# Two transformer blocks on one core: new order of VectorE's and ScalarE's work between stages and at the entry of the HGRN stage

## What is computed

```python
h = norm(x) * (1.0 + scale) + shift        # layer_norm behind stages 0 and 1, rms_norm behind 2 to 6
# stage 0: token_mixer (sparse attention and convolution), then layer_norm(ALPHA * x + gate * y)
# stage 1: swiglu, then layer_norm(ALPHA * x + gate * y)
# stages 2, 4, 5, 7: x + 0.5 * gate * ((silu(h @ w_a) * (h @ w_b)) @ w_down)
# stage 3: x + gate * diff_attention(h);  stage 6: x + gate * hgrn2(h)
```

## Time and profile before

| | us |
|---|---|
| median of 3 runs | 1468.14 (1464.91 to 1470.73) |
| profiled execution | 1470.92 |
| its span, first to last instruction | 1469.2 |
| mean granted TensorE clock | 0.979 of full |

### The profile page before, as it was taken

The page is one execution under the profiler, slowest core; times in us unless marked ns, Lnnn a source line. Parts: engine busy times, 40 slices in busy tenths (PEclk is TensorE's granted clock), DMA queues, the critical chain, the costliest instruction groups (busy, mean ns, idle before and its releaser), DMA issues.

```text
span 1469.2 us, 19939 instructions
## 1 busy us (share of the span) xinstructions
PE 1425.0 (97%) x7214; PEld 1194.3 (81%) x7214; DVE 1061.4 (72%) x1133; ACT 693.4 (47%) x897; POOL 183.4 (12%) x273
## 2 busy tenths in 40 slices
PE   8998899999899999999999999999999999899998
PEld 8897788888788888767788887888888988788887
DVE  5888867775678877776667775688866888755555
ACT  2452354343444435666644345534347856544342
POOL 3103211110301210221101101111101001100000
PEclk7996999999999999999999999999999999999999
DMA  9836478986389995532589983899955342366761
GB/s 354 316 138 201 145 257 308 314 308 213 100 294 341 374 379 170 174 138 91 176 274 313 313 281 111 285 335 341 342 177 171 116 141 87 129 201 211 231 225 62
DMA packets 187528, 335.64 MB, mean 228 GB/s; under 512 B 9170, under 2 KB 123454, under 8 KB 187217
## 3 DMA queue, kind: packets, MB, share of 16 engines
q1 hardware_dynamic: 160528, 237.95, 48.1%
q0 software_dynamic: 26736, 96.71, 18.3%
q10 hardware_dynamic: 208, 0.23, 0.0%
HBM read 332.23 MB, written 2.63 MB: 228 GB/s over the span
## 4 chain that ended last, share of the span: by engine, by line
PE 79%; DVE 10%; issue 4%; ACT 3%; POOL 1%; DMA 1%; SPq 1%; DVEq 0%; ACTq 0%; POOLq 0%
PE ps L2087 70%; DVE wlo L1259 2%; PE ps L2279 1%; PE ps L2095 1%; PE ps L2540 1%; POOL st L492 1%; DVE ada_acc L1560 1%; PE ps L2210 1%; DVE xn L1321 1%; DMA big<-in_w_ada 1%; DVE xs L1327 1%; ACT whi L672 1%; PE ps L2638 0%; PE ps L2755 0%; ACT xn L712 0%
## 5 line engine op out<-in xcount | busy, mean ns | idle before, releaser
L1259 DVE TENSOR_TENSOR wlo<-raw,whi 128x2048 fp32r<-128x2048 f32 x206 | 470.2, 2285 | 153.5 <-ACT whi L672 152.3
L672 ACT ACTIVATE whi<-raw 128x2048 fp32r<-128x2048 f32 x215 | 409.7, 1909 | 213.9 <-PE ps L2087 158.2
L2087 PE MATMUL ps<-whi,hhi 128*128 128x512 f32 (+1 forms) x1208 | 491.2, 407 | 15.7 <-DVE hlo L1307 5.5
L2087 PE MATMUL ps<-whi,hlo 128*128 128x512 f32 (+1 forms) x1208 | 476.4, 394 | 0.0
L2087 PE MATMUL ps<-wlo,hhi 128*128 128x512 f32 (+1 forms) x1208 | 475.9, 394 | 0.0
L2087 PEld LDWEIGHTS ps<-whi,hhi 128*128 128x128 f32 x1208 | 230.2, 191 | 67.8 <-issue 10.2
L2087 PEld LDWEIGHTS ps<-whi,hlo 128*128 128x128 f32 x1208 | 230.0, 190 | 49.6
L2087 PEld LDWEIGHTS ps<-wlo,hhi 128*128 128x128 f32 x1208 | 230.4, 191 | 45.1 <-issue 1.7
L2087 PE MATMUL ps<-whi,ahi 128*128 128x512 f32 x400 | 156.1, 390 | 0.0
L2087 PE MATMUL ps<-whi,alo 128*128 128x512 f32 x400 | 155.7, 389 | 0.0
L2087 PE MATMUL ps<-wlo,ahi 128*128 128x512 f32 x400 | 155.7, 389 | 0.0
(11 more groups left out here) (287 smaller groups left out, 1494.9 us busy)
## 6 DMA issues: line engine op xcount, KB each, us to landing
raw<-in_ffn_w_in SPq DMA_DIRECT2D x176, 512.0 KB
ada_raw<-in_ada_w POOLq DMA_DIRECT2D x96, 512.0 KB, 5.1
raw<-in_ffn_w_down SPq DMA_DIRECT2D x44, 1024.0 KB
big<-in_ada_w POOLq DMA_DIRECT2D x48, 512.0 KB, 6.3
raw<-in_hgrn_w_in SPq DMA_DIRECT2D x16, 1024.0 KB
raw<-in_attn_w_qkv SPq DMA_DIRECT2D x12, 1024.0 KB
ada_raw<-in_w_ada POOLq DMA_DIRECT2D x23, 512.0 KB, 5.0
raw<-in_w_gate SPq DMA_DIRECT2D x22, 512.0 KB
```

Of the source, the lines that this page charges most:

```text
L672: sc.activation(whi[:, slot, 0:n], raw[:, slot, 0:n], ACT.Copy).then_inc(w_hi, 1)
L1259: ve.tensor_tensor(wlo[:, slot, 0:n], raw[:, slot, 0:n], whi[:, slot, 0:n].bitcast(F32), ALU.subtract)\
L2087: done = pe.matmul(dst, lhsT, rhs, start=first and n == 0, stop=final and n == 2, skip_group_check=True)
```

## The change

- Border of stages 1 and 2: the column sums of stage 2 leave the last gate-up product of stage 1 and take the place of 16 filler products behind `close`; `leave_second` is a new order for VectorE, with the layer norm's first passes ahead of the wait for the root; the mean for the root is added on VectorE for both halves (`whole_mean`); ScalarE makes the high part of the second unit ahead of the squares and modulates all eight tiles in both halves.
- All borders: ScalarE alone modulates the second half, all eight tiles. `SHARED` lists the halves that stay divided.
- Borders from 2 on: the high parts of border units come in halves (`hi_half`) at other places in ScalarE's order, TensorE waits for low parts in halves (`lo_first`, then `w_lo`).
- Stages 3 and 6: the first transposes of the next stage go ahead of the last down product of half 1 instead of into its middle.
- Entry of stage 6: ScalarE makes two high parts first, then copies the gate row, then the exponential. VectorE makes two low parts ahead of `bounds`.
- Filler products in `enter`: 16 at stage 2 before the second transposes (9 and 8 around them before), 5 or 1 instead of 7 at the others.

The lines of the diff, with most of the context left out:

```diff
+SHARED = tuple((s, 0) for s in (1, 3, 4, 5, 6, 7))
+HALVED = [FIRST[s] + g for s in range(3, NSUB) for g in range(2) if g or s in (4, 7)]
...
     def inverse_rms(s, t):
         mean = st[:, 1 + 2 * t:2 + 2 * t]
-        if t:
-            pool.wait_ge(mean_eps, s)
+        if t or s == 1:
+            pool.wait_ge(mean_eps, s + t)
             inverse_root(mean, 1, rms_root)
             return
         pool.wait_ge(sums_s, 4 * (s - 1) + 2)
...
             sc.wait_ge(w_used, used(unit - RING, lap))
         sc.activation(whi[:, slot, 0:n], raw[:, slot, 0:n], ACT.Copy).then_inc(w_hi, 1)
+    h_mod_s_count = [NT]
+    def hi_half(unit, h):
+        slot, cols = unit % RING, slice(h * D, (h + 1) * D)
+        if h == 0:
+            sc.wait_ge(w_land[slot], 32 * (unit // RING + 1))
+            sc.wait_ge(w_used, used(unit - RING))
+        sc.activation(whi[:, slot, cols], raw[:, slot, cols], ACT.Copy).then_inc(w_hi if h else hi_first, 1)
     def modulate(s, t):
-        sc.wait_ge(h_tr, 4 * s + 2 * t + 2)
         toks = slice(t * P, (t + 1) * P)
+        shared = (s, t) in SHARED
         for g in range(2):
-            for kt in (4 + 2 * g, 5 + 2 * g):
-                done = sc.activation(hf[:, kt, toks], ps[:, 2 * t + 1, (kt - 4) * P:(kt - 3) * P], ACT.Identity,
+            if shared:
+                kts = (4 + 2 * g, 5 + 2 * g)
+                if g == 0:
+                    sc.wait_ge(h_tr, 4 * s + 2 * t + 2)
+            else:
+                kts = range(4 * g, 4 * g + 4)
+                sc.wait_ge(h_tr, 4 * s + 2 * t + g + 1)
+            for kt in kts:
+                done = sc.activation(hf[:, kt, toks], ps[:, 2 * t + kt // 4, kt % 4 * P:(kt % 4 + 1) * P], ACT.Identity,
                                      scale=modc[:, s % 2, 8 + kt:9 + kt], bias=modc[:, s % 2, kt:kt + 1])
-            if g == 0:
-                sc.wait_ge(h_mod_v, 2 * s + t + 1)
+            if g == 0 and shared:
+                sc.wait_ge(h_mod_v, NT + SHARED.index((s, t)) + 1)
             else:
                 done.then_inc(h_mod_s, 1)
-                sc.wait_ge(h_mod_s, 2 * s + t + 1)
+                h_mod_s_count[0] += 1
+                sc.wait_ge(h_mod_s, h_mod_s_count[0])
             sc.activation(hhi[:, 4 * g:4 * g + 4, toks], hf[:, 4 * g:4 * g + 4, toks], ACT.Copy).then_inc(h_hi, 1)
     def split_mixed(n, k0, k, t0, tn):
...
     def leave(s):
         n = s + 1
-        if s:
-            for h in range(2):
-                square(s, 0, h)
+        if s == 0:
+            normalised(0)
+            sc.wait_ge(cols_set, n + 1)
+            modulate(n, 0)
+            hi(FIRST[n] + 1)
+            normalised(1)
+        else:
+            if s == 1:
+                hi(FIRST[n] + 1)
+            square(s, 0, 0)
+            square(s, 0, 1)
             if s not in SWIGLUS:
-                hi(FIRST[n])
+                hi_half(FIRST[n], 0)
             scaled(s, 0)
-        else:
-            normalised(0)
-        sc.wait_ge(cols_set, n + 1)
-        modulate(n, 0)
-        hi(FIRST[n] + 1)
-        if s:
+            if s not in SWIGLUS:
+                hi_half(FIRST[n], 1)
+            elif s > 1:
+                hi_half(FIRST[n] + 1, 0)
+            sc.wait_ge(cols_set, n + 1)
+            modulate(n, 0)
+            if s not in SWIGLUS:
+                hi_half(FIRST[n] + 1, 0)
             square(s, 1, 0)
+            if s not in SWIGLUS:
+                hi_half(FIRST[n] + 1, 1)
             square(s, 1, 1)
+            if s in SWIGLUS and s > 1:
+                hi_half(FIRST[n] + 1, 1)
             scaled(s, 1)
-        else:
-            normalised(1)
         modulate(n, 1)
-        if n not in LATE_GATES:
+        if n not in LATE_GATES and n != 6:
             set_gate(n)
     def swiglu(s):
...
+        hi(U + 2)
+        hi(U + 3)
+        set_gate(6)
...
-        hi(U + 2)
-        hi(U + 3)
...
     def lo_half(unit, h):
...
-        ve.wait_ge(w_hi, used(unit))
-        done = ve.tensor_tensor(wlo[:, slot, cols], raw[:, slot, cols], whi[:, slot, cols].bitcast(F32), ALU.subtract)
-        if h:
-            done.then_inc(w_lo, 1)
+        if h == 0 and unit in HALVED:
+            ve.wait_ge(hi_first, HALVED.index(unit) + 1)
+        else:
+            ve.wait_ge(w_hi, used(unit))
+        ve.tensor_tensor(wlo[:, slot, cols], raw[:, slot, cols], whi[:, slot, cols].bitcast(F32), ALU.subtract)\
+            .then_inc(w_lo if h else lo_first, 1)
...
     def lo(unit, lap=0, n=UNIT):
...
+    def join(t, h):
+        cols = slice(h * BANK, (h + 1) * BANK)
+        link(ve.scalar_tensor_tensor(xs[:, t, cols], xs[:, t, cols], ALPHA, xn[:, t, cols], ALU.mult, ALU.add))
+    def moments(t, h):
+        at = 12 + 12 * t + 6 * h
+        link(ve.bn_stats(st[:, at:at + 6], xs[:, t, h * BANK:(h + 1) * BANK]))
     def half_moments(s, t, h):
-        x_h, y_h = gated(s, t, h)
-        link(ve.scalar_tensor_tensor(x_h, x_h, ALPHA, y_h, ALU.mult, ALU.add))
-        at = 12 + 12 * t + 6 * h
-        link(ve.bn_stats(st[:, at:at + 6], x_h))
+        gated(s, t, h)
+        join(t, h)
+        moments(t, h)
...
     def last_moments(s, t):
...
+        deviation(t)
+    def deviation(t):
...
     def layer_norm(t):
...
-        ve.wait_ge(ln_root, 2 + t + 1)
...
+        ve.wait_ge(ln_root, 2 + t + 1)
+        for h in range(2):
+            x_h = xs[:, t, h * BANK:(h + 1) * BANK]
...
-        modulate(1, 1)
...
-    def second_mean(s):
-        ve.wait_ge(sums_s, 4 * s)
-        ve.tensor_scalar(st[:, 3:4], st[:, 3:4], st[:, 253:254], EPS2, ALU.add, ALU.add).then_inc(mean_eps, 1)
+    def whole_mean(s, t):
+        ve.wait_ge(sums_s, 4 * (s - 1) + 2 * t + 2)
+        mean = st[:, 1 + 2 * t:2 + 2 * t]
+        ve.tensor_scalar(mean, mean, st[:, 251 + 2 * t:252 + 2 * t], EPS2, ALU.add, ALU.add).then_inc(mean_eps, 1)
+    def leave_second():
+        n = 2
+        half_moments(1, 0, 0)
+        last_moments(1, 0)
+        layer_norm(0)
+        gated(1, 1, 0)
+        whole_mean(1, 0)
+        join(1, 0)
+        moments(1, 0)
+        set_columns(n)
+        lo_half(FIRST[n], 1)
+        gated(1, 1, 1)
+        rest_of_input(n, 0, 0)
+        join(1, 1)
+        moments(1, 1)
+        deviation(1)
+        rest_of_input(n, 0, 1)
+        layer_norm(1)
+        lo_half(FIRST[n] + 1, 0)
+        whole_mean(1, 1)
+        ve.wait_ge(rms_root, 2)
+        lo_half(FIRST[n] + 1, 1)
...
     def conclude(s):
...
                     residual(s, t, h)
             return
         if s == 1:
-            half_moments(1, 0, 0)
-            last_moments(1, 0)
-            layer_norm(0)
-            lo_half(FIRST[n], 1)
-            half_moments(1, 1, 0)
-            ve.wait_ge(cols_set, n + 1)
-            modulate(n, 0)
-            rest_of_input(n, 0, 0)
-            last_moments(1, 1)
-            rest_of_input(n, 0, 1)
-            lo(FIRST[n] + 1)
-            layer_norm(1)
-            second_mean(s)
+            leave_second()
         else:
             residual(s, 0, 0)
             residual(s, 0, 1)
             if s in SWIGLUS:
                 lo_half(FIRST[n], 1)
+                gated(s, 1, 0)
             else:
                 set_columns(n)
-                lo(FIRST[n])
+                lo_half(FIRST[n], 0)
             ve.wait_ge(cols_set, n + 1)
             modulate(n, 0)
-            gated(s, 1, 0)
-            rest_of_input(n, 0, 0)
-            add_gated(1, 0)
+            if s in SWIGLUS:
+                add_gated(1, 0)
+                rest_of_input(n, 0, 0)
+            else:
+                lo_half(FIRST[n], 1)
+                rest_of_input(n, 0, 0)
+                residual(s, 1, 0)
             residual(s, 1, 1)
             rest_of_input(n, 0, 1)
+            whole_mean(s, 1)
+            ve.wait_ge(rms_root, RMS_ROOT[s] + 2)
             lo_half(FIRST[n] + 1, 0)
-            second_mean(s)
-            ve.wait_ge(rms_root, RMS_ROOT[s] + 2)
             lo_half(FIRST[n] + 1, 1)
-        modulate(n, 1)
         rest_of_input(n, 1, 0)
         rest_of_input(n, 1, 1)
...
-            set_columns(s + 1)
+            if s > 1:
+                set_columns(s + 1)
...
+        lo(U + 3)
...
-        for j in range(3, 6):
-            lo(U + j)
+        lo(U + 4)
+        lo(U + 5)
...
         slot = unit % RING
-        if t == 0:
+        in_halves = t == 0 and inputs is not None and inputs > 1
+        if in_halves:
+            pe.wait_ge(lo_first, 2 * (inputs - 2) + g + 1)
+        elif t == 0:
             pe.wait_ge(w_lo, used(unit, lap))
         if inputs is not None:
             pe.wait_ge(h_lo, (4 * inputs + 2 * t + g if inputs else 2 * g + t) + 1)
         for k in range(4):
             kt = 4 * g + k
+            if in_halves and k == 2:
+                pe.wait_ge(w_lo, used(unit))
             tok_cols = slice(t * P, (t + 1) * P)
             done = three(ps[:, b, 0:n], hhi[:, kt, tok_cols], hlo[:, kt, tok_cols],
```

(19 more changed lines are left out.)

3 lines of the change are left out of this document (1 added, 2 removed).

## The result

The changed kernel takes 1455.13 us (median of 6, 1453.74 to 1459.57) against 1469.24 (6 runs, 1464.91 to 1471.82) for the kernel before: a ratio of 0.991, interval 0.9891 to 0.9929. A second set of 6 runs on another chip gave 1453.44 against 1467.40 (11 runs), 0.9906 (0.9879 to 0.9932). The forecast was 1454.9, and both intervals lie under 0.995, the forecast's line for "faster". The profiled execution took 1458.36 (span 1456.7), before 1470.92 (1469.2).

The account below looks back on a forecast made before the run. TensorE, busy 97% of the span, was taken as the bound, with loss at stage borders that are chains over the other engines. Terms summed to 13.25 us, giving 1454.9 from a median of 1468.14; range 1450 to 1460.5.

Parts of the forecast that it names:

- Column sums: Last gate-up of stage 1: 9.61 us falls to 5.92, and the sums cost nothing in place of filler; -3.7 us.
- 1 to 2: Border of stages 1 and 2: second scaling starts 3.5 us earlier, chunk 1 at 398.5 for 402.30; -3.8 us.
- 2 to 3 and 4 to 5: These two borders: halved high parts bring scaling 1.4 us earlier, eight tiles on ScalarE give part back; -0.6 us each.
- 5 to 6: Entry of stage 6: transposes 1.4 us earlier, TensorE's 1.26 us wait for the third unit's low part goes; -2.65 us.
- rival (b): Stages 2, 3 and 6 swallow much of the border gains through loads and their own chains: 1459.5 us; chance 0.12.
- 3 to 4 and 6 to 7: Entries of stages 4 and 7: 1.27 us gaps go by earlier transposes and halved high parts; -0.8 and -1.1 us.
- (a): Idle TensorE at border 1 to 2 lowers the granted clock, costing 1.7 to 2.5 us: 1457 to 1459; chance 0.12.
- (c): Five borders from 2 to 3 on: ScalarE becomes the bound, each pays 1.0 and 1.55 us: 1480 us; chance 0.04.
- (d): Whole kernel: only the column sums count, the rest hides behind other waits: 1464.4 us; chance 0.04.

Follow-up runs that it names:

- x1: Kernel before, with only stage 2's column sums moved from stage 1's last gate-up to the place of 16 filler products: 1463.85 us against 1467.2.
- x8: Changed kernel with both halves of the second unit's low part ahead of the second layer norm at border 1 to 2: 1454.28 us.
- x2: Changed kernel with the second token half's modulation shared by VectorE (tiles 0 to 3) and ScalarE (4 to 7) again: 1456.26 us.
- x3: Changed kernel with high parts in one piece again at borders from 2 to 3 on, at their old places in ScalarE's order: 1458.94 us.
- x6: Changed kernel with the attention bias transfers on GpSimd's queue moved from stage 2's loop into stage 1's: 1450.24 us.
- z1: Changed kernel with ScalarE making the gate of stages 2, 3 and 5 after the high halves instead of ahead of them: 1453.73 us.
- x5: Changed kernel with the first transposes of stages 4 and 7 back inside the last down product of half 1: 1456.31 us.
- x7: Changed kernel without the 16 filler products ahead of stage 2's second transposes: 1455.26 us.
- z0: Changed kernel run again without any edit, on the same chip as z3: 1453.44 us, ratio to the kernel before 0.9906.
- x4: Changed kernel with stage 6's old entry order: gate row, table load and exponential ahead of the third and fourth high part: 1462.39 us.
- z3: Changed kernel with the edits of x6 and z1 and the filler of z4 together: 1452.48 us, ratio to the kernel before 0.9894.
- z4: x5 with 14 filler products on TensorE behind the last head turns of stage 6: 1461.92 us.

## Why the prediction was right

**Column sums, -3.7.** Measured -3.70, and x1 shows it alone. The comparison of stage 1 with stage 7 inside one trace was exact.

**1 to 2, -3.8.** Measured -3.41. Every step of the second half has the forecast length: scaling to gate copy 5.61 (5.6), gate copy to chunk 1 5.52 (5.5), the eight tiles with copies 4.2 (4.3). The missing 0.4 is earlier: the first scaling came 0.67 earlier instead of 1.0, and the second scaling at 14.9 for a forecast 14.6. Up to the start of chunk 1 the terms are: second scaling 3.17 earlier (forecast 3.5), of which x8 gives the low part 2.02 (forecast 1.8); transposes another 1.18 closer to it, since before the change they started 1.96 behind the scaling, after products at the low clock of the earlier trace rows and filler, and now 0.78; less 0.89 for eight tiles in place of four. That makes 3.46. x2 shows the price of the tiles alone, 0.86: the shortening comes in spite of it. The Trainium skill (ScalarE: Activation LUTs, Rules for kernel authors) would keep multiply and add on VectorE. At 1 to 2 the trace agrees (43.90 with VectorE's share, 44.76 without), at stage 6 it doesn't (84.65 against 84.09): the queue decides, not the 0.13 us between the two rows.

**2 to 3 and 4 to 5, -0.6 each.** Measured -0.67 and -0.70; x3 shows that they hang on the halves (1.55 and 1.57). The scaling at 2 to 3 starts 16.93 behind the last turn and not 18.47, which is 1.54 for a forecast 1.4, and ScalarE's idle time before it (0.91 in the earlier trace rows) is gone. The unknown in the sum, the 128x1024 high part put at 1.0, measures 1.04 in the changed kernel.

**5 to 6, -2.65.** Measured -3.03. The step was right and a little small; the wait for the low part is gone. It reaches the next stage whole: every later wait of stage 6 that the two kernels share stands 3.0 earlier behind the last turn of stage 5, up to the one of 1.63 us near its end, against rival (b).

**3 to 4 and 6 to 7, -0.8 and -1.1.** The gaps of 1.27 became 0.24 and 0.19. With like clock the end of stage 3 shortens by 0.67 (x1 54.93 from the last wait for `hf` to stage 4's first turn, x6 54.26), and the end of stage 6 by 0.8 (from the wait of 1.63 us to stage 7's first turn 37.55 before and 36.79 in z1, both at 0.91). The rest of the two rows of 1.0 in the table is the clock's. Part of what the first transposes gain goes back at the second: their wait grew from 0.59 to 1.10, where the forecast had its end 0.8 earlier. x5 says what the placement is worth, 1.4 at 3 to 4. The forecast gave two causes here, the placement and the halves of the high part; by x3 the halves do nothing at these two borders, so this half of its reason was wrong.

**The sum.** 3.70+3.41+0.67+0.67+0.70+3.03+0.8=12.98 for a forecast of 13.25. The medians differ by 14.1, the profiled spans by 12.6: 12.98, less the 1.50 of stage 2, plus 1.1 of start-up and clock. The terms are shown at their borders. That the total came within 0.3 us of the median is luck: terms were off by up to 0.4 with both signs, the profiled execution carried 1.5 in stage 2 that no term had, and the interval of the ratio leaves room for 10.4 to 16.0 us.

**The rivals.** (a) didn't occur at the border it named, but x7 and x8 bring it about at once, and the clock scatters elsewhere. (b) named stage 2, which was 1.5 longer in the profile; that the change caused it isn't shown, and at stages 3 and 6 nothing was swallowed. (c) appears only when the halves are taken away. (d) is refuted by every border, and by x1: alone, the sums are 3.7 of the 13.

## What to carry to other kernels

Cost a border as a chain from one start to the next, each with its length from a like instruction of the trace, and compare runs by such stretches; the time of one run here moves by more than most edits. An engine's order at a border is worth more than the speed of its instructions: one low part behind layer norm gave 2.0 us, one gate copy and table load behind two high parts 2.3, and one gate copy more in the tail another 0.9. Before moving work to another engine, look at what queue it escapes: at the same two instructions' cost the move lost 0.86 at one border and won 0.56 at another.

## What the runs showed of the hardware

The granted clock of TensorE varies from run to run at the same instructions behind the same waits. I had the clock as a risk of new gaps; it was in the kernel before all along (0.83 over 10 us in stage 3, 0.91 over 20 us at the end of stage 6), at places where TensorE waits once or twice for some 1 to 2 us. Ten microseconds from the end of the 1.73 us wait in stage 3, in the changed kernel and in z0, which is the same kernel:

```profile
671.28:681.28 10.00, 10.00 (x52) 8.42 (x53) 6.94 (x12) 7.57 (x22) 0.58 (x2) 1.00 0.34 105
```

```profile
669.77:679.77 10.00, 10.00 (x45) 8.32 (x46) 6.18 (x12) 6.43 (x18) 0.00 (x0) 0.83 0.34 105
```

Such a drop costs about 1.5 us here: from stage 2's last turn to stage 4's first x4, with 0.83, takes 162.99, and x6 to x8, with 1.00, take 161.45 to 161.50. What it costs hangs on the waits behind it. From the wait of 1.29 us in stage 6 to stage 7's first product the changed kernel takes 19.12 with the clock full over 20 us, z0 19.43 with 0.91 and x4 20.74 with 0.84: the first is cheap, since the slower products use up the wait of 0.93 us, which of the runs without filler there only those with the full clock have. The place where it varies most is ahead of stage 1. Window 120 to 150 us of the changed kernel, then of x8, whose code differs only behind stage 1:

```profile
120.00:150.00 30.00, 27.81 (x109) 23.58 (x109) 23.75 (x37) 7.24 (x8) 11.68 (x11) 0.60 0.60 198
```

```profile
120.00:150.00 30.00, 26.65 (x113) 22.49 (x113) 26.12 (x38) 7.80 (x8) 13.26 (x14) 0.73 0.70 241
```

Stage 1's first turn is at 197.4 to 198.1 us in six runs with 0.59 to 0.60 (before, after, x4, z0, z3, z4), at 195.2 in z1 with 0.62, and at 192.4 to 194.3 in seven with 0.69 to 0.77 (x1, x2, x3, x5 to x8). That is 3 to 6 us for code that is nearly the same in all, as much as the largest edit of this change, and it is the largest single difference between the profiled executions. Of the other executions only time and mean granted clock are on record. They point the same way: of z0's six, two with 0.979 took 1460.2 and 1461.0, and four with 0.985 to 0.987 took 1450.2 to 1455.1. The Trainium skill (TensorE: Matmul & The Clock Gate, What's actually happening) says that the monitor behind the clock runs freely and doesn't start with the kernel; the runs are in keeping with it, though they can't prove it: the same gap in stage 3 costs 1.5 us in z0 and x4 and nothing in x6 to x8.
